# Hybrid decoder layer with PEER experts: the turn of the expert choices two blocks earlier, 24 gathered items up to block 52 and 25 in the last pass

## The reference

```python
def peer_ffn(x, wq, subkeys, u, v):
    q = (xt @ wq).reshape(n, PEER_HEADS, 2, PEER_DQ // 2)
    s = jnp.einsum('nhpd,pkd->nhpk', q, subkeys)
    sv, si = lax.top_k(s, PEER_TOPK)                       # 16 of 128 keys, on each of two sides
    cand = sv[:, :, 0, :, None] + sv[:, :, 1, None, :]
    cs, ci = lax.top_k(cand..., PEER_TOPK)                 # 16 of the 256 sums
    eidx = ...                                             # expert = key of side 0 * 128 + key of side 1
    gate = jax.nn.softmax(cs, axis=-1)
    hid = jax.nn.gelu(jnp.einsum('cd,chkd->chk', xc, u[ec]))
    return jnp.einsum('chk,chkd->cd', gc * hid, v[ec])     # 8 heads x 16 experts of 16384 for each token
```

## Time and profile before

| | us |
|---|---|
| median of 3 runs | 1789.9 |
| the runs | 1789.77, 1789.9, 1794.04 |
| the profiled execution | 1790.11 |
| its span | 1788.3 |

### The profile page before, as it was taken

One profiled execution on the slowest core, in us unless ns is written; L12 is line 12 of the kernel. 1 busy time (PEld: TensorE's weight loads), 2 busy tenths in 40 slices (PEclk: granted clock), 3 DMA queues, 4 the chain that ended last, 5 costly groups with the idle time before them and its releaser, 6 DMA issues.

```text
span 1788.3 us, 28007 instructions
## 1 busy us (share of the span) xinstructions
PE 1768.8 (99%) x10676; PEld 1586.1 (89%) x10676; DVE 1417.8 (79%) x2185; ACT 784.5 (44%) x1070; POOL 177.4 (10%) x158
## 2 busy tenths in 40 slices
PE   8999999999999999999999999999999999999998
PEld 8899989889999999999977777789999997777775
DVE  6546667566988957877678899889999998999996
ACT  5334444655321011111655555555555555555555
POOL 0000000000000111212011010211111101111110
PEclk9999999999999999999999999999999999999999
DMA  9774544556546987989889999999999999999984
GB/s 354 257 284 150 165 142 142 188 188 224 170 162 218 355 311 294 358 334 351 316 307 390 340 345 351 347 356 369 373 374 376 372 365 351 362 374 379 358 308 153
DMA packets 77616, 532.66 MB, mean 298 GB/s; under 512 B 8827, under 2 KB 9227, under 8 KB 16604
## 3 DMA queue, kind: packets, MB, share of 16 engines
q1 hardware_dynamic: 54656, 378.75, 57.2%
q0 software_dynamic: 22544, 152.38, 23.4%
q10 hardware_dynamic: 332, 0.44, 0.1%
HBM read 513.38 MB, written 15.99 MB: 296 GB/s over the span
## 4 chain that ended last, share of the span: by engine, by line
PE 97%; DVE 1%; issue 1%; ACT 0%; DMA 0%; SPq 0%; DVEq 0%
PE bank L937 16%; PE bank L957 12%; PE bank L603 8%; PE bank L604 8%; PE bank L605 8%; PE bank L1031 7%; PE bank L1030 6%; PE bank L1035 6%; PE bank L1036 6%; PE bank L1037 6%; PE bank L958 6%; PE bank L987 2%; PE bank L750 0%; DMA hT<-in_xT 0%; PE bank L924 0%
## 5 line engine op out<-in xcount | busy, mean ns | idle before, releaser
L1330 ACT ACTIVATE hi<-raw 128x1024 fp32r<-128x1024 f32 x400 | 422.3, 1060 | 344.5 <-PE bank L1037 252.7
L1968 DVE TENSOR_TENSOR lo<-raw,hi 128x1024 fp32r<-128x1024 f32 x400 | 483.2, 1222 | 109.7 <-ACT hi L1330 109.3
L957 PE MATMUL bank<-xr,hi 128*128 128x384 f32 x1152 | 328.7, 359 | 1.0 <-DVE xr L1981 1.0
L937 PE MATMUL bank<-hT,raw 128*128 128x192 f32 x1792 | 295.7, 326 | 0.0
L937 PEld LDWEIGHTS bank<-hT,raw 128*128 128x128 f32 x1792 | 290.6, 190 | 0.0
L958 PE MATMUL bank<-xr,lo 128*128 128x192 f32 x1152 | 288.4, 250 | 0.0
L1468 DVE TENSOR_TENSOR lo<-raw,hi 128x2048 fp32r<-128x2048 f32 x75 | 171.8, 2291 | 90.4 <-ACT hi L1099 68.1
L958 PEld LDWEIGHTS bank<-xr,lo 128*128 128x128 f32 x1152 | 220.0, 191 | 0.1
L957 PEld LDWEIGHTS bank<-xr,hi 128*128 128x128 f32 x1152 | 216.5, 188 | 2.1 <-DVE xr L1981 2.0
L1031 PE MATMUL bank<-lo,wm 128*64 128x512 f32 x512 | 202.8, 396 | 0.0
L1030 PE MATMUL bank<-hi,wm 128*128 128x512 f32 x512 | 199.7, 390 | 1.0 <-DVE wm L2031 0.6
(11 more groups left out here) (292 smaller groups left out, 2622.9 us busy)
## 6 DMA issues: line engine op xcount, KB each, us to landing
raw<-in_u SPq DMA_DIRECT2D x128, 1024.0 KB
raw<-in_v SPq DMA_DIRECT2D x128, 1024.0 KB
raw<-in_w_in SPq DMA_DIRECT2D x43, 1024.0 KB
raw<-in_w_out SPq DMA_DIRECT2D x16, 1024.0 KB
raw<-in_wq SPq DMA_DIRECT2D x16, 1024.0 KB
gate_matrix<-gs POOLq DMA_DIRECT2D x12, 832.0 KB, 11.6
gs<-gate_matrix SPq DMA_DIRECT2D x13, 768.0 KB, 11.0
raw<-in_cmp_w SPq DMA_DIRECT2D x8, 1024.0 KB
```

The costliest lines, as they stand in the source:

```text
L937: last = mm(bank[s % 2][:, 0:TD], raw[:, s, k * P:(k + 1) * P], xn[:, k, 0:TD], start=(k == 0), stop=(k == KT - 1))
L957: mm(acc_bank[:, 0:2 * TD], hi[:, s % 2, w], xr[:, k, :], start=(k == 0), stop=False, skip_group_check=True)
L1330: do(hi[:, s % 2, cols], raw[:, s, cols], ACT.Copy).then_inc(v_hi_ready, 1)
L1968: vec.tensor_tensor(lo[:, n % 2, cols], raw[:, n % RAW, cols], hi[:, n % 2, cols].bitcast(F32), ALU.subtract).then_inc(v_lo_ready, 1)
```

## The change

ROUTED goes from 28 to 26: PE turns the choices behind 26 blocks (26 is no multiple of the loop's four blocks, so blocks 24 and 25 are written out behind the loop), ACT copies them behind block 26, and the gate products stand behind blocks 27 to 50 where they stood behind 29 to 52. ACT's exponential moves from block 23 to 22 (EXP_DENSE). The first 12 items are due over blocks 10 to 25 where it was 10 to 27, the next stage (ROUTED to 51) has 24 items where it had 22, and the last one 25 where it had 27. EARLY_SPLIT is 8 on both sides.

```diff
-ROUTED = 28
+ROUTED = 26
...
-EXP_SPARSE, EXP_DENSE, PAIRS_LISTED = 8, 23, 10
+EXP_SPARSE, EXP_DENSE, PAIRS_LISTED = 8, 22, 10
...
-STAGE_ITEMS = ((PAIRS_LISTED, ROUTED, FIRST_GATHERS), (ROUTED, 52, 22), (HALF, 2 * HALF, 29),
-               (2 * HALF, 3 * HALF - 3, 38), (3 * HALF, 4 * HALF - 10, 27))
+STAGE_ITEMS = ((PAIRS_LISTED, ROUTED, FIRST_GATHERS), (ROUTED, 52, 24), (HALF, 2 * HALF, 29),
+               (2 * HALF, 3 * HALF - 3, 38), (3 * HALF, 4 * HALF - 10, 25))
...
             with pe.Fori(1, ROUTED // RAW) as lap:
                 for s in range(RAW):
                     u_block(RAW * lap + s, s)
+            for r in range(ROUTED // RAW * RAW, ROUTED):
+                u_block(r, r % RAW)
```

## The result

| | before | changed |
|---|---|---|
| median of 20 runs, us | 1790.49 | 1794.36 |
| lowest to highest | 1789.16 to 1794.04 | 1789.66 to 1798.52 |
| mean | 1790.65 | 1793.82 |
| runs over 1795 | 0 | 7 |

The ratio is 1.0018 with a 95% interval of 1.0012 to 1.0025: slower by some 3.2 us (the medians are 3.9 us apart), inside 0.3%. The lowest times are half a microsecond apart; what changed is how far the others lie above them (standard deviation 2.6 us where it was 1.2).

The account below looks back on a forecast made before the run. PE bounds the kernel, busy 1768.8 of 1788.3 us, with at most 5.0 us to gain. Terms 2.4 + 0 + 0 + 0 on the profiled 1790.11 give 1792.5, as a median 1792.3 us (+0.13%); range 1789.4 to 1795.6.

Parts of the forecast that it names:

- The turn: Behind block 26, before the transposes: PE waits 2.4 us for the choices, the term that counts.
- a transposes' row without idle: Sign at L978: about 2.2 us of idle expected; none would make the claimed wait for the choices wrong.
- first step: Behind block 26: PE arrives at 657.95, choices are ready at 660.25, so PE waits 2.4 us with the hand-over.
- The bounds of 0 to 4.9: PE's wait behind block 26: 0 without DVE's last 3.47 us wait, 4.9 us if the last two gathers come 2.5 later.
- The due times bind nowhere: First 12 gathers: earlier due times find the same two full buffers and change nothing; choices stay at 660.25.
- The clock: Rival: PE's clock falls to half after the wait behind block 26, losing 3.6 us more, 1795.9 us; 7%.
- Batches, stores, items: Gate batches and 24 items of the next stage move together by two blocks: 0, ends -0.6 and +2.4 us.
- The late store: Gate store issued at 748.99, landing after 14.0 us against a median of 11.6; counted unchanged, same queue in front.
- The tail: Three items behind the last batch, the third done at 850.2: cost 0, upper end +2 us; as deciding rival 8%.
- the hole at batch 12: PE lost 0.62 us there to a late store and ACT's late copy; counted as unchanged.
- The last pass: Two items fewer relieve nothing; the 0.61 us hole behind v block 49 stays: 0, with -0.6 as an end.
- the clock case: Rival: the wait behind block 26 halves PE's clock; 2.4 + 3.6 = 6.0 us give 1795.9 us; 7%.

Follow-up runs that it names:

- the table: Six profiled executions with the turn at 26, 12 items in front and no filler, of the changed kernel and variants; own times 1789.75 to 1796.10 us.
- e2: Against the kernel before, only the turn, its copy and the exponential moved two blocks up; batches and items unmoved: 1793.10 us, ratio 1.0013.
- e5: Changed kernel with the turn behind 27 blocks (ROUTED = 27): 1791.62 us, ratio 1.0002.
- e6: Changed kernel with 10 items and not 12 in front of the choices, 27 in the last pass: 1791.21 us, ratio 1.0000.
- e4: Against the kernel before, only the items per stage changed; turn and batches unmoved: 1790.26 us, ratio 0.9999.
- e11: One more profiled execution of the kernel before, no edit: 1791.38 us.
- e7: Changed kernel with the turn behind 24 blocks and the exponential at 20: 1805.83 us, ratio 1.0070.
- e3: Against the kernel before, turn and gate batches moved, items per stage left at 22 and 27: 1792.92 us, ratio 1.0017.
- e10: One more profiled execution of the changed kernel, no edit: 1791.61 us.
- e1: The changed kernel again, no edit: median 1793.87 us, ratio 1.0016 against the kernel before; its profiled execution took 1795.9 us.
- the first group: Four kernels timed on one chip: the changed one again and three that split its change; medians 1790.26 to 1793.87 us.

## Why the prediction was right, and where not

**The turn: right mechanism, a sum from one draw.** Idle of PE before L978, released by DVE's L1923, is what the three executions of the table above 1793 us have, and e2, e5 and e6 tie the loss to it. The step said 2.4 us from "the value of the very rows". It was one draw (660.25) of a quantity that spreads over 7 us. PE arrives at 657.9 to 659.3, so the wait is 0 in some executions and 3.6 in others; half of the six above have none, which by the prediction's own sign (a transposes' row without idle) contradicts its first step. The bounds of 0 to 4.9 held every one. That the sum came close was luck in part: over the six the idle is 1.4 us in the mean for the 2.4 forecast, and 0.9 us of clock, put at nothing in the sum, make it 2.3.

**The due times bind nowhere.** Right by the traces: in the four executions that still have the old ones (before, e2, e4, e11) POOL began the last gather at 645.5 to 646.7, some 3 us or more behind the end of the block that it also waits for (about 642.4), and in e7, whose due times are earlier again, the choices came at 662.30. One thing stays open: in those four the choices came at 660.25 to 661.39, and the four early ones (655.87 to 657.59, in the changed kernel, e3, e5 and e10) all have earlier due times. No wait explains that, and twelve executions are too few to tell it from chance.

**The clock: given 7% as a rival, and it is part of the usual case.** The step failed in making it all or nothing and rare. In every profile with an idle of 2.21 us or more (four) the clock fell to half; and it cost 1.7 to 2.2 us, not the 3.6 taken from the whole 7.1 us at the start, since the level came back about 4 us after PE had resumed (in e1 PE resumes at 662.81, and the granted clock is 0.50 at 664 to 666 and 1.00 from 667). An execution of the table that waits pays 3.9 to 5.3 us for both, one that doesn't pays nothing. Over the six in the table that is 2.3 us in the mean, against 3.2 over the timed runs of the result and 2.6 over the 36 of the first group: six are too few to say whether the rest is chance, and this stays open. (The reading of the start rests on the matmuls' durations; the granted clock in the profile's rows says 1.00 there.) On the rule of the Trainium skill that was weighed ("TensorE: Matmul & The Clock Gate", section "HAM oscillation — how this bites in real kernels"), the trace agrees in kind: the bursts behind the idles of 2.21 to 3.58 us ran at half the clock at first, and the wait cost 1.7 us more than its length.

**Batches, stores, items: 0, as said.** e4 at 0.9999 confirms it for the items, and e3 beside e2 for the batches (1.0017 and 1.0013, not told apart). The late store was not tied to its place in the queue, though: it took 12.3 us in the profile after for 14.0 in the one before, and the hole from a late copy stood at other batches in other executions (0.99 us at 750.89 in e11, the kernel before; 0.57 us at 824.48 in e10).

**The tail.** The cost of 0 was right and its working was off: the third item was worked off at 843.60 and not at 847.8. Of that, 3.3 us were there before the first of the three, nearly all because this execution has neither the wait at the turn (2.4) nor the hole at batch 12 (0.6); the rest is mostly there because the gather was quicker than the 8.2 us that it was sized by (7.5 us; the one before it took 10.5). What came last there was SP's load of the first split block, which no step had named; PE's 1.0 us stayed.

**The last pass.** The hole of 0.6 us stayed, as said, in every profile here.

**The range** held the median, 1794.36, and the outcome is inside 0.3% as forecast; the forecast itself, 1792.3, was 2.1 us low. The range was said to take in nearly all of the clock case, but that case's own 1795.9 lies above its end of 1795.6, and single executions went up to 1798.52.

## What to carry to other kernels

Before a wait is moved in front of an engine that is never idle, read when its releaser comes in several executions, not in one: the slack of one trace (here 8.1 us) is one draw if what it depends on is a chain of gathers that spreads over 7 us. On TensorE the waits of 2.21 to 3.58 us cost their length and 1.7 us for the clock here, so even useless work put into such a wait cost nothing; an execution that would not have waited pays for all of it. And when only the spread of a kernel grows while its fastest time stays, as here, look for a race between two chains before you look for added work.

## What the runs showed of the hardware that was not expected

- An idle of 2.21 us on TensorE was followed by the clock at 1.2 GHz (e2, granted clock 0.50 in 662 to 663). The longest idle in the middle of a program without a fall was 1.78 us (e5, granted clock 1.00 in every microsecond from 784 to 794). After idles of 2.2 to 3.6 us the fall came after the work had resumed. In e7, with 13.52 us of idle, it came during it: 1.00 in 648 to 653 and 0.51 in 653 to 662.
- Each fall cost 1.7 to 2.2 us, whatever the idle before it (2.21 to 13.52 us).
- The gather of the twelfth item, the last in front of the choices, kept DVE waiting between 0.7 us (e11) and 5.5 us (e7) over the executions.
